# The down projection of two blocks as seven products of half matrices in place of eight

## What is computed

```python
def merge_and_ffn(x, attn, conv, g, w_out, ..., w_ffn_gate, w_ffn_up, w_ffn_down, g_post_ffn):
...
    h = rmsnorm(x, g_pre_ffn)
    f = (jax.nn.silu(h @ w_ffn_gate) * (h @ w_ffn_up)) @ w_ffn_down
    return x + rmsnorm(f, g_post_ffn)
```

## Time and profile before

| | |
|---|---|
| median of 3 runs | 2989.41 us (2988.89 to 2991.73) |
| the profiled execution, its own time | 2988.57 us |
| its span in the trace | 2986.8 us |
| PE busy | 2932.4 us, 98% of the span |
| DVE, ACT, POOL busy | 68%, 49%, 23% |
| granted PE clock | 1.00 in all stages below, that is 2.4 GHz |

### The profile page before, as it was taken

One profiled execution on the slowest core, in us unless ns is written; L12 is line 12 of the kernel. 1 busy time (PEld: TensorE's weight loads), 2 busy tenths in 40 slices (PEclk: granted clock), 3 DMA queues, 4 the chain that ended last, 5 costly groups with the idle time before them and its releaser, 6 DMA issues. The chain is left out here.

```text
span 2986.8 us, 50911 instructions
## 1 busy us (share of the span) xinstructions
PE 2932.4 (98%) x18791; PEld 2618.2 (88%) x18791; DVE 2030.7 (68%) x3674; ACT 1451.5 (49%) x2877; POOL 680.0 (23%) x658
## 2 busy tenths in 40 slices
PE   8999999999999999999999999999999999999998
PEld 7777789988888889998888888999899999899976
DVE  8998779874797747663398775665369867466623
ACT  5766555554455535553155544554225554455412
POOL 4950035520581000000086000000039400100001
PEclk9999999999999999999999999999999999999999
DMA  8875746678654355556655444556565443445543
GB/s 297 274 244 200 268 146 210 206 280 300 223 190 166 128 187 166 179 182 226 218 195 185 142 156 158 188 186 210 196 208 173 169 132 121 170 157 172 178 168 122
DMA packets 204454, 573.44 MB, mean 192 GB/s; under 512 B 24000, under 2 KB 26816, under 8 KB 203696
## 3 DMA queue, kind: packets, MB, share of 16 engines
q1 hardware_dynamic: 191728, 548.81, 54.2%
q10 hardware_dynamic: 12480, 21.38, 1.9%
HBM read 456.03 MB, written 114.16 MB: 191 GB/s over the span
## 5 line engine op out<-in xcount | busy, mean ns | idle before, releaser
L1325 PE MATMUL PS<-h_hi,w_hi 128*128 128x512 f32 (+2 forms) x1664 | 533.4, 353 | 9.0 <-DVE u L2710 5.4
L1325 PE MATMUL PS<-h_hi,w_lo 128*128 128x512 f32 (+2 forms) x1664 | 525.3, 349 | 0.0
L1325 PE MATMUL PS<-h_lo,w_hi 128*128 128x512 f32 (+2 forms) x1664 | 525.3, 348 | 0.0
L1355 PE MATMUL PS<-op_hi,w_hi 128*128 128x256 f32 x1680 | 476.6, 284 | 2.2 <-DVE w_lo L2429 2.2
L1355 PE MATMUL PS<-op_lo,w_hi 128*128 128x256 f32 x1680 | 475.4, 283 | 0.0
L1355 PE MATMUL PS<-op_hi,w_lo 128*128 128x256 f32 x1680 | 475.4, 283 | 0.0
L1221 POOL TENSOR_TENSOR y<-y,prod 128x512 f32<-128x512 f32 (+1 forms) x333 | 431.8, 1325 | 157.9 <-ACT prod L1947 144.9
L2314 DVE SCALAR_TENSOR_TENSOR PS<-u,dw,PS 128x512 f32<-128x512 f32 (+1 forms) x604 | 434.1, 766 | 7.0
L2429 DVE TENSOR_TENSOR w_lo<-raw,w_hi 128x512 fp32r<-128x512 f32 x376 | 287.8, 775 | 155.1 <-ACT w_hi L1799 154.3
L1325 PEld LDWEIGHTS PS<-h_hi,w_hi 128*128 128x128 f32 x1664 | 293.9, 188 | 53.3 <-issue 13.1
L1325 PEld LDWEIGHTS PS<-h_hi,w_lo 128*128 128x128 f32 x1664 | 294.0, 188 | 39.3
(11 more groups left out here) (316 smaller groups left out, 5864.0 us busy)
## 6 DMA issues: line engine op xcount, KB each, us to landing
w_lo<-lo_dram SPq DMA_DIRECT2D x240, 512.0 KB, 4.5
w_hi<-hi_dram SPq DMA_DIRECT2D x240, 512.0 KB, 3.6
raw<-in_w_stream SPq DMA_DIRECT2D x292, 256.0 KB, 3.4
w_raw<-sum_dram SPq DMA_DIRECT2D x180, 256.0 KB, 3.0
w_raw<-in_w_stream SPq DMA_DIRECT2D x80, 512.0 KB, 5.2
hi_dram<-w_hi SPq DMA_DIRECT2D x80, 512.0 KB, 5.6
lo_dram<-w_lo SPq DMA_DIRECT2D x80, 512.0 KB, 3.7
sum_dram<-raw ACTq DMA_DIRECT2D x60, 256.0 KB, 2.3
```

The costliest lines, as they stand in the source:

```text
L1325: last = nc.tensor.matmul(PS[:, k0 + off, col:col + n], w, x[:, k, c0:c0 + n], start=first and k == 0, stop=stop and k == KT - 1)
L1355: last = nc.tensor.matmul(out, w[:, part_k], o[:, k, :], start=start and first and k == 0, stop=stop and k == KH - 1, skip_group_check=again)
```

## The change

In blocks 1 and 2 (`SEVEN`) the down projection is done by the scheme of seven products of half matrices. The 512 tokens, the 22 tiles of hidden features (even and odd ones) and the 1024 output columns are cut in two each; a product i of 1 to 7 is a sum over e = 0 to 10 of *pieces* (i, e) of 128 hidden features, 256 tokens and 512 columns: 2 token tiles x 3 = 6 matmuls of 512 columns. `passes` sets the order of the 77 pieces, numbered v: products 1 and 5 in turn (v = 0 to 21), 2 and 6, 4 and 7, then 3 alone. In what follows a piece of a product of `KEPT` (1, 2, 3) takes weights as they were stored, half a row of `hi_dram` and one of `lo_dram` (256 KB each); the pieces of the other products take a sum of weights from the new `t_dram` (256 KB), which ACT and DVE split in each of the two blocks.

- POOL makes those sums once, in block 1 while PE does gate and up (`sums_of_weights`): in each of 11 rounds it issues 4 loads of 256 KB, does 8 operations of 256 elements, and issues 2 stores of 512 KB, in a buffer `t_sum` in the place of the last three tiles of `f`. ACT waits for the last store before it writes tile FT - 3 = 19 of `f`.
- POOL makes the sums of activations in place in `f`, 44 of them in each of the two blocks (`sum_of_pieces`), nine pieces ahead.
- ACT and DVE split the pieces of activations (256 elements) five pieces ahead into a ring of six, and the summed weights in a ring of seven places (eight from v = 49).
- The products are put together in PSUM (products 6 and 7 are added in the bank of product 1, which ACT copies out three times, `hold`) and by five additions of DVE on 1024 elements.
- The work on the next block's tiles stands at pieces 3, 6, 10, 13, 17, 20, 24, 27 and 31 (`STEP_END`) in place of steps 0 to 8.
- Residuals of token tiles 0 and 1 are added before the end of the stage, those of 2 and 3 behind it.

The diff, cut to its core:

```diff
+SEVEN = (1, 2)
+MAKES_T = SEVEN[0]
+KEPT = (1, 2, 3)
+X2, Z2, Y2, W2 = 2, 4, 6, 0
...
+def passes():
+    order = []
+    for lead, other in ((1, 5), (2, 6), (4, 7)):
+        order += [(lead, 0), (lead, 1)]
+        for e in range(HALF_D - 2):
+            order += [(lead, e + 2), (other, e)]
+        order += [(other, HALF_D - 2), (other, HALF_D - 1)]
+    return order + [(3, e) for e in range(HALF_D)]
+DOWN = passes()
+ND7 = len(DOWN)
+DSLOT = {ie: n for n, ie in enumerate(DOWN)}
+PLACE = [v % 7 if v < 49 else (v - 49) % 8 for v in range(ND7)]
+FR = 6
+DAHEAD = 5
+SUM_AHEAD = 9
+SUMS_F = [(i, e) for i in (5, 6, 7, 3) for e in range(HALF_D)]
+SUM_POS = {ie: n for n, ie in enumerate(SUMS_F)}
+STEP_END = [-(-7 * (dd + 1) // 2) - 1 for dd in range(FT)]
...
+        t_sum = at("t_sum", R_g + (FT - 3) * TX * 4, [P, 2, 2, 2, T // 2])
...
+        def place_free(eng, b, v):
+            before = [u for u in range(v) if PLACE[u] == PLACE[v]]
+            if before:
+                down_used(eng, b, before[-1])
+            else:
+                unit_used(eng, b, NU - 8 + PLACE[v])
...
+        def f_piece(v):
+            i, e = DOWN[v]
+            return {1: first_half(e, 0), 2: first_half(e, 1), 3: first_half(e, 1), 4: second_half(e, 1),
+                    5: second_half(e, 0), 6: first_half(e, 0), 7: second_half(e, 0)}[i]
...
+            def down_units(b):
+                k = 0
+                for v, (i, e) in enumerate(DOWN):
+                    place_free(sp, b, v)
+                    if i in KEPT:
+                        s = S_D + e + (HALF_D if i == 3 else 0)
+                        cols_of = slice(0, HW) if i == 1 else slice(HW, 2 * HW)
+                        if b == SEVEN[0]:
+                            sp.wait_ge(hi_out[s % HI], 16 * (s // HI + 1))
+                            sp.wait_ge(lo_out[s % LO], 16 * (s // LO + 1))
+                        sp.dma_start(down_high(v).bitcast(F32), hi_dram[s, :, cols_of]).then_inc(rawq_in[PLACE[v]], 16)
+                        sp.dma_start(down_low(v).bitcast(F32), lo_dram[s, :, cols_of]).then_inc(rawq_in[PLACE[v]], 16)
+                    else:
+                        half, odd = {5: (0, 0), 4: (0, 1), 7: (1, 0), 6: (1, 1)}[i]
+                        sp.dma_start(down_raw(v).rearrange("p (c n) -> p c n", c=2),
+                                     t_dram[e, :, :, half, odd, :].rearrange("c p n -> p c n")
+                                     ).then_inc(rawq_in[PLACE[v]], 16)
+                    for dd in steps_at(v - DAHEAD):
+                        if dd % 2 and (dd + 1) // 2 < tiles(b + 1):
+                            load_x(b + 1, (dd + 1) // 2)
...
+            def sums_of_weights():
+                pool.wait_ge(op_ok, len(OPS) * (MAKES_T + 1))
+                made = len(SUMS) * NP
+                for e in range(HALF_D):
+                    for n in range(2):
+                        if e == 0:
+                            load_of_sums(e, n)
+                        elif n == 0:
+                            load_of_sums(e, 0)
+                            load_of_sums(e, 1)
+                    for n in range(2):
+                        b11, b21, b12, b22 = (t_sum[:, n, half, odd, :] for half in range(2) for odd in range(2))
+                        pool.wait_ge(t_in[n], 32 * (e + 1))
+                        nc.gpsimd.tensor_tensor(b11, b12, b11, ALU.subtract).then_inc(ws_ok, 1)
+                        pool.wait_ge(ws_ok, made + 1)
+                        nc.gpsimd.tensor_tensor(b12, b22, b12, ALU.subtract).then_inc(ws_ok, 1)
+                        pool.wait_ge(ws_ok, made + 2)
+                        nc.gpsimd.tensor_tensor(b22, b22, b11, ALU.subtract).then_inc(ws_ok, 1)
+                        pool.wait_ge(ws_ok, made + 3)
+                        nc.gpsimd.tensor_tensor(b21, b21, b22, ALU.subtract).then_inc(ws_ok, 1)
+                        made += 4
+                        pool.wait_ge(ws_ok, made)
+                        pool.dma_start(t_dram[e, n], t_sum[:, n]).then_inc(t_out[n], 16)
+            def load_of_sums(e, n):
+                if e:
+                    pool.wait_ge(t_out[n], 16 * e)
+                cols_of = slice(n * T // 2, (n + 1) * T // 2)
+                for half in range(2):
+                    src = w_stream[S_D + 2 * FT + half * HALF_D + e].rearrange("p (k n) -> p k n", k=2)
+                    pool.dma_start(t_sum[:, n, half], src[:, :, cols_of]).then_inc(t_in[n], 16)
...
+                    if s == S_D and seven(b):
+                        sums_for(b, 0, SUM_AHEAD)
+                        for v in range(ND7):
+                            sums_for(b, v + SUM_AHEAD, v + SUM_AHEAD + 1)
+                            for dd in steps_at(v):
+                                start, _, _ = s0_at(S_D + dd, b)
+                                if start is not None:
+                                    inv_rms(b + 1, start, 0)
...
+            def down_of_seven(b):
+                for v, (i, e) in enumerate(DOWN):
+                    if i in KEPT:
+                        down_landed(pe, b, v)
+                    else:
+                        pe.wait_ge(weight_low_ok, 1 + raw_units(b, v))
+                    low_piece_made(pe, b, v)
+                    k = {1: X2, 6: X2, 7: X2, 5: Z2, 2: Y2, 3: Y2, 4: W2}[i]
+                    if e == 0:
+                        if i in (1, 5, 2):
+                            for bank in (k, k + 1):
+                                out_made(pe, b, *last_read(bank))
+                        elif i == 4:
+                            pe.wait_ge(hf_ok, first_norm(b + 1, tiles(b + 1) - 1) + 1)
+                        elif i == 3:
+                            combined(pe, b, 1)
+                        else:
+                            pe.wait_ge(copies_ok, 1 + 3 * sevens_before(b) + (1 if i == 6 else 2))
+                    hi, lo = down_high(v), down_low(v)
+                    for t in range(2):
+                        x_hi, x_lo = (d[:, v % FR, t * P:(t + 1) * P] for d in (d_hi, d_lo))
+                        for x, w, start, stop in ((x_hi, hi, True, False), (x_hi, lo, False, False),
+                                                  (x_lo, hi, False, True)):
+                            last = nc.tensor.matmul(PS[:, k + t, :], x, w, start=start and e == 0 and i not in (6, 7),
+                                                    stop=stop and e == HALF_D - 1, skip_group_check=i in (6, 7))
+                        if t == 0 and v in W_USED_AT:
+                            last.then_inc(w_used, 1)
+                    last.then_inc(w_used if v == ND7 - 1 else dm_used, 1)
...
+                i, e = DOWN[v]
+                if v < FR:
+                    finished(act, b, (FT - 1, 2))
+                else:
+                    down_used(act, b, v - FR)
+                if (i, e) in SUM_POS:
+                    sum_made(act, b, (i, e))
+                elif i in (1, 4):
+                    up_out(act, b, e)
+                A(d_hi[:, v % FR, :], f_piece(v), ACT.Copy).then_inc(fhi_ok, 1)
+                if i not in KEPT:
+                    down_landed(act, b, v)
+                    place_free(act, b, v)
+                    A(down_high(v), down_raw(v), ACT.Copy).then_inc(weight_high_ok, 1)
...
+            def down_of_seven(b):
+                for v, (i, e) in enumerate(DOWN):
+                    high_piece(b, v + DAHEAD)
+                    if i in (1, 6, 7) and e == HALF_D - 1:
+                        hold(b, v)
+                    for dd in steps_at(v):
+                        start, _, out = s0_at(S_D + dd, b)
+                        if out is not None:
+                            normed_hi(b + 1, out)
+                        if start is not None:
+                            sum_squares(b + 1, start, 0)
...
+                    if b == MAKES_T and j == FT - 3:
+                        for n in range(2):
+                            act.wait_ge(t_out[n], 16 * HALF_D)
...
+                dve.wait_ge(fhi_ok, pieces_before(b) + v + 1)
+                TT(d_lo[:, v % FR, :], f_piece(v), d_hi[:, v % FR, :].bitcast(F32), ALU.subtract).then_inc(flo_ok, 1)
+                if DOWN[v][0] not in KEPT:
+                    dve.wait_ge(weight_high_ok, 1 + raw_units(b, v))
+                    TT(down_low(v), down_raw(v), down_high(v).bitcast(F32), ALU.subtract).then_inc(weight_low_ok, 1)
...
+            def down_of_seven(b):
+                for v, (i, e) in enumerate(DOWN):
+                    low_piece(b, v + DAHEAD)
+                    if e == HALF_D - 1:
+                        if i == 2:
+                            down_used(dve, b, v)
+                            dve.wait_ge(copies_ok, 1 + 3 * sevens_before(b) + 1)
+                            TT(stash_of(b, 1), two_banks(Y2), stash_of(b, 1), ALU.add).then_inc(c_ok, 1)
+                        elif i == 6:
+                            dve.wait_ge(copies_ok, 1 + 3 * sevens_before(b) + 2)
```

(21 more changed lines are left out.)

215 lines of the change are left out of this document (181 added, 34 removed).

## The result

The changed kernel takes 3037.5 us (median of 4 runs, 3035.0 to 3040.2) against 2990.6 us of the kernel before on the same chip: ratio 1.0155, 95% interval 1.0138 to 1.0173. It is 47 us slower, where I had forecast no change (2986.5) and a range up to 3012.

The account below looks back on a forecast made before the run. PE bounds the kernel, busy 2932 of 2987 us. Terms -30.0 + 15.8 + 4.0 + 1.5 + 2.0 + 3.8 + 0 = -2.9 us on 2988.57 gave 2985.7, as median 2986.5; range 2968 to 3012.

Parts of the forecast that it names:

- What is removed: Down projections of blocks 1 and 2: 528 matmuls become 462, saving 15.0 us each, 30.0 us if PE never waits.
- The waits of the down stage: PE waits at low parts of pieces because DVE is in a 6.24 us chain: 7.9 us a block, 15.8 for both.
- SP's hold: Down stage: SP stands at tile loads waiting for `h_lo`, delaying weight loads behind; PE waits 0.9 and 0.2 us.
- POOL's lock: Down stages: DVE waits for POOL's operations, two hits of 0.35 on each of three chains, 4 us for both blocks.
- The clock: Read as 1.00 (2.4 GHz) throughout gate and up of block 1 and its down projection; no term in the sum.
- my rivals: Late sums 3008 (25%); covered chains 2973 (20%); nothing given back 2959 (5%); down stage gives back more 2998 (12%).
- The sums of weights: Gate and up of block 1: 11 POOL rounds of 15.1 us take 169 us, just in time, so 0 us.
- The estimate of 3.2 us for a store: From the skill page's DMA fit: a store 3.2 us, a round 14.8 with 1 us for an issue.
- late sums: Rival, 25%: rounds over 15.1 us make ACT stand at j = 19 and PE starve; at 17.3, 22 us: 3008.
- POOL beside gate and up: Gate and up of block 1: POOL's 88 operations (66 us) beside it cost 1.5 us (0 to 2.6).
- Stage start: Down stage start: first summed weights' place, ACT and DVE wait behind loads; 0 to 3 us a block, 2 for both.
- Stage end: End of block 2's down stage: late residuals of tiles 2 and 3 cost 3 us, next first weights 0.8; 3.8.

Follow-up runs that it names:

- f1: e12 with POOL's 88 sums of activations on one column in place of 256 (output not the reference's): 2966.3 us, ratio 0.9926.
- e2: Changed kernel with PE's transposes of the next block's tiles two pieces later: 3037.7 us, ratio 1.0168.
- e5: Changed kernel, ACT summing the next tile's squares before the previous tile's high part, DVE's normed_lo one piece later: 3034.5 us, ratio 1.0150.
- e10: Changed kernel with e6's buffer places, e5's order and the squares' scratch output in tmp instead of PSUM: 3002.3 us, ratio 1.0040.
- e9: e6 with the loads of the next block's tiles from 2 on issued by ACT in place of SP: 3008.6 us, ratio 1.0057.
- e11: The edits of e9 and e10 together: 2991.3 us, ratio 1.0004.
- e12: e6 with the parts of the step on a tile spread over pieces, each tile seven pieces behind the one before: 2981.1 us, ratio 0.9964.
- e1: Changed kernel without POOL's sums of weights, plain weights loaded in place of t_dram (output not the reference's): 3011.0 us, ratio 1.0078.
- e4: Kernel before the change, with eight waits of PE put into the down projections of blocks 1 and 2: 3041.0 us, ratio 1.0178.
- e3: Changed kernel with POOL's 88 sums of activations on one column in place of 256 (output not the reference's): 3021.4 us, ratio 1.0113.
- e6: Changed kernel with the sums-of-weights buffer in the two places of the next block's tiles, not in f: 3015.8 us, ratio 1.0080.
- f4: e12 with the sums of weights begun earlier and the transposes and what follows a piece later: 2982.9 us, ratio 0.9973.

## Why the prediction was wrong

In sum: the two down stages took 268.3 us, and PE's own work in them is 219.8 (twice 109.9, f1). So 48.5 us were given back there, 32.7 as waits and the rest as longer busy time, where my sum had 21.8 (15.8 + 4.0 + 2.0). Gate and up of block 1 gave back 21.4 where I had 1.5 + 0. The forecast failed at the waits of the down stage, at the clock and at the round of the sums of weights. Term by term:

- **What is removed, 30.0 us: right within 2 us.** PE's busy time in a down stage at clock 1.00 is 109.9 (f1, both blocks) against 123.7 and 124.4: 13.8 and 14.5 us.
- **The waits of the down stage, 7.9 us a block: right chain, wrong size and place.** I placed three waits of 1.15, 2.55 and 3.1 us at low parts. There were waits of 4.23, 2.96 and 3.83 at transposes in block 1, and five in block 2: with `w_lo` 12.7 and 20.0 us. The place was wrong in the step "PE wants it after 7 pieces and one tile's transposes": I counted the transposes as 0.79 us of work and did not ask what they wait for, which is `scale_rows`, in the same chain. But the place is not what cost: with the transposes two pieces later the waits were 14.5 and 19.5 us (e2). The size was wrong because the things that make DVE late were under-priced: the chain, where one pair of PSUM banks in place of two ties each tile's squares to the tile before (taking this out, in the order of e5, gave 5.0 and 6.8 us, e10), and SP's hold and POOL's lock, which follow below. I also took block 2, whose next block has a fifth tile, as equal to block 1.
- **SP's hold: seen, priced too low.** It was to cost 0.9 and 0.2 us. It was 6.9 to 8.6 us long at each load, and taking it away gave 4.4 us a stage (e9), 7.7 in block 2 with the squares' tie gone (e10 to e11).
- **The clock: missing from the sum.** That "the clock is 1.00 (2.4 GHz) throughout" was a row of before, and I carried it over to a kernel with waits. PE was busy for 12.0 us more in the down stages than in e12, 2.7 more in gate and up (229.45 against 226.72), and some 1.7 us lie at the start of block 3: 16 us. These are an account of busy time and not what a full clock alone would win: in e1 PE was busy for 3.7 us less in one down stage, and the stage was no shorter. Only in e4, where nothing else was late, is it a price. All of my rivals' prices lacked it as well.
- **The sums of weights, 0 us: the round was mis-sized.** 16.5 us in place of 15.1. Four issues stand in a round's chain, two loads and two stores, and took 2.6 us (2 x 0.73 + 2 x 0.58), where I had 3.2; the store's landing behind its issue took 4.0 in place of 4.3, two more loads' issues included; the operations with their handovers 8.3 in place of 7.6. The landing of the loads, 5.5 us, was not in the round at all: POOL waited 20.0 us for it in 11 rounds, 1.8 each. The estimate of 3.2 us for a store, worked out beside the sum, was too low. The rival "late sums" is what happened, but that its 22 us match the measured 21.4 is in part luck: it had them for a round of 17.3, and by its rule a round of 16.5 gives 14. Measured are a wait of 18.7 and 2.7 of half clock.
- **POOL's lock, 4.0 us: 12 to 13** (e3, f1). I counted two hits on three chains; it costs DVE 14 to 18 us in each stage, spread over its operations, in a stage in which DVE is the second longest.
- **POOL beside gate and up, 1.5 us:** the changed kernel has no wait of PE there that the one before lacks, but for the one for ACT, and e1, without the sums, has the length of before. With the buffer elsewhere the stage took 227.5 (e12) to 233.5 us (e10, e11); this spread stays open in part.
- **Stage start, 2.0:** no wait was there. **Stage end, 3.8: right**, a wait of 3.74 at step 1 of block 3, where I had 3.0 for it and 0.8 for the first weights; the half clock behind it was not in it. Landings from `t_dram` were 3.4 us against 3.25.

The lengths of operations that nothing held and the landings from `t_dram` were good; lacking were what makes DVE late (a shared bank pair, SP's hold, POOL's lock on every operation) and the price of a wait.

## What to carry to other kernels

When a stage gets shorter, list for every engine what stands between two of its deadlines, PE's own small operations among them, and ask of each what it waits for: a step that was hidden behind 5.5 us of matmuls is not hidden behind 1.4. Price a wait of PE of over some 3 us at its length plus 2.5, and do not count a shorter one as free of it: here some waits of 2 us had 3.4 us at half clock behind them. Look first at ways that break a serial chain over engines into parts several pieces apart. Here this and another place for a buffer turned 47 us lost into 11 won with the work of every engine unchanged; the place gave some 22 of these 58, the spread step the others. Scratch outputs and buffers "in the place of" something carry dates: squares in a shared bank pair and sums in the room of `f` cost more than their work.

## What was not expected of the hardware

- With PE waits of 3.13 to 10.33 us the granted clock fell to 0.50 for 3.4 to 10.2 us, part of it still in the wait; behind 1.25 and 2.19 us it did not (e4). Other runs have the clock fall behind 1.97, 1.99 and 2.02 us (e6, f4, e9) and stay behind 3.08 and 3.33 (e1, e10). In e12 no wait in the two blocks' stages was over 1.64 us, and the clock stayed at 1.00 in them.
- A DMA issue took POOL 0.73 us for a load in runs of 1 KB and 0.58 for a store of 512 KB; SP's issues mostly take 0.32 to 0.43.
- A POOL operation held DVE's `tensor_scalar` on one tensor (754 to 1215 ns) as it holds those with two.
- With 293 GB/s in gate and up of block 1 (187 before), SP's loads of 256 KB took 4.3 and 5.0 us to land in place of 2.8 and 3.7, and PE still had no new wait there but the one for ACT.
